# A hybrid decoder trunk on one NeuronCore: three HGRN weight blocks as three float32r products in place of one float32 product, and new rooms for the first projection weights

## The chip, the core and the metric

The kernel runs on one core of a Trainium2 chip. TensorE (PE) multiplies, VectorE (DVE) and ScalarE (ACT) do elementwise work, GpSimd (POOL) and SyncE (SP) issue most of the DMAs. The metric is the device time of one execution in microseconds (us), the median of several runs.

## The reference

Two layers of a decoder trunk for 320 tokens (256 of one prompt, 64 of eight samples), 1024 channels, float32. Each layer is a first feed-forward block, a mixer and a second feed-forward block:

```
x += 0.5 * post1(SwiGLU1(pre1(x)))
x += postm(Mix(prem(x)))
x += 0.5 * post2(SwiGLU2(pre2(x)))

Mix(u):  proj = u @ w_in                       # columns: A, B, C and three merge gates
  oa = rwkv7(A)      # 8 heads of 64, handled as 4 pairs
  ob = rglru(B)      # scan
  oc = hgrn2(C)      # 4 heads of 128, chunked, norm, gate
  merged = ga*(oa @ proj_a) + gb*(ob @ proj_b) + gc*(oc @ proj_c)
  return merged @ w_out
```

## The kernel before

All activations are kept transposed, as eight tiles of 128 channels by 320 tokens. The weights are packed in the order of use into blocks of 128 x 2048 float32 (1 MB), `wstream`; 110 blocks a layer. Blocks 0 to 33 are the first feed-forward layer, 34 to 41 the input columns of RWKV, 42 to 53 those of RG-LRU and HGRN, 54 to 57 and 58 to 65 (`B_G0`, `B_G1`) the merge gates, 66 to 71 (`B_PROJ`) the three branch projections, 72 to 75 `w_out`, 76 on the second feed-forward layer. Two SBUF buffers, `raw0` for even and `raw1` for odd blocks, take turns; SP loads a block as soon as its buffer is given back.

A block is multiplied in one of two ways. In the *float32* way (`pieces`, L607) a tile is one float32 matmul straight from `raw` and the normed input `u`; the trace records each such matmul as two. In the *float32r* way the weight and the input are each split into a high part (a copy rounded to float32r) and a low part (the difference), and a tile is three float32r matmuls: high by high, high by low, low by high. ACT makes a high part by a Copy, DVE a low part by a subtraction. The feed-forward layers, the RWKV columns, the projections and `w_out` go this way with both parts made just before use (L703, L557).

Eleven of the twelve blocks of RG-LRU and HGRN columns, the *turn* blocks (`turn_pieces`, L642), go this way with a detour. Their low parts are made during the first feed-forward layer, half a block at a time: POOL loads a half into `u` (free then), ACT makes the high part in `wha` (`presplit_hi`), DVE the low part over it (`presplit_lo`), and POOL stores that in DRAM, in `split_store`. In the mixer SP loads a raw half (512 KB) into the lower half of a `raw` buffer and the stored low half (512 KB) beside it, ACT turns the raw half into the high part in place (`turn_high`), and PE multiplies. A half's buffer is reloaded when PE has done the half, so at most two halves, one in each buffer, are there. The inputs' high parts are `nh` (it lies over `x`, which waits in DRAM meanwhile), the low parts `nl`, six tiles in `wha` and two in `ovr`.

The mixer's work on PE is interleaved by hand: `dense_part(n)` issues n tiles of weight product between the small matmuls of the recurrences. During the four HGRN heads (`hgrn_head`) these are the eight blocks 58 to 65, two a head, 16 tiles a block, all in the float32 way. In heads 0 to 2 they are issued in runs of 3, 1, 1, 1, 1, 2, 2, 2, 2, 3, 1, 2, 1, 1, 3 and 6 tiles, in head 3 in runs of 3, 1, 1, 1, 1, 2, 2, 2, 2, 3, 3 and 11. In a head's first part seven level steps alternate: DVE scales operands (`factors`), PE multiplies them (L917), DVE keeps a masked part of the result (`keep`, L1927). Then come a transposition (L922), state products (L933), the output (L947), a norm (L951), and the next head's first transposes (L906).

After head 3 PE goes on with the projections, in halves of a block (`high` on ACT, `low_half` on DVE, L557 on PE). The split parts of each half have a *room* in SBUF by a table, `half_homes`; the first four halves, 14 to 17, of blocks 66 and 67, use (`WB0`,`LO`), (`WB1`,`SS`), (`WA0`,`U0`), (`WA1`,`U1`). `WA` is in `wha`, which is also the HGRN state buffer `hs`/`hsn`; `WB` is `whb`, which is also the small weights `sw`; `U` is in `u`; `LO` is in the last tiles of `ov`; `SS` is the RWKV state buffer.

Of the kernel before, what the change touches and what calls it, by code (L numbers as in the profile page):

```python
# [70 lines left out]
NLOAD = (NBLK - (B_G0 - B_B)) // 2  # L71
# [75 lines left out]
def trunk(nc, xT, wstream, smallw, params, logits, consts, st_shift, st_rwkv, st_lru, st_conv, st_hgrn,  # L147
          yT, o_shift, o_rwkv, o_lru, o_conv, o_hgrn):
    ctx = ExitStack()
    with ctx:  # L150
# [12 lines left out]
        split_store = nc.dram_tensor("split_store", (L * NSPLIT, P, 1024), F32).ap()  # L163
# [20 lines left out]
        rt = sb("rt", T)  # L184
        rs = sb("rs", T)
# [101 lines left out]
        nl = [wha[:, T * k:T * k + T] for k in range(6)] + [ovr[:, 0, :], ovr[:, 4, :]]  # L287
# [10 lines left out]
        def split_half(h):  # L298
# [10 lines left out]
        block_done full_done half_done half_hi half_lo branch_hi branch_lo merged_hi merged_lo x_new x_first uh_first u_first sq_ready sq_added sq_last first_done hi_ready lo_ready uh_ready sum_done rt_ready u_ready u_half u_full nh_ready nl_ready x_spilled x_back turn_done turn_hi presplit silu_ready h_ready  # L309
# [14 lines left out]
        pre_loaded, pre_hi, pre_lo, pre_stored, turn_loaded, low_loaded = (  # L324
            [sem(f"{n}{h}") for h in range(2)]
            for n in ("pre_loaded", "pre_hi", "pre_lo", "pre_stored", "turn_loaded", "low_loaded"))
# [32 lines left out]
        def wait_full(eng, l, j):  # L359

            eng.wait_ge(S["full_done"], l * (B_PROJ - B_G0) + (j - B_G0 + 1))

        def wait_turn(eng, l, g):

            eng.wait_ge(S["turn_done"], l * NTURN + (g + 1))

        def landed(l, pair):

            return (l * NLOAD + pair - ((B_G0 - B_B) // 2 if 2 * pair >= B_G0 else 0)) * 16 + 16

# [10 lines left out]
        def _(sp):  # L381
# [18 lines left out]
            for l in range(L):  # L400
# [17 lines left out]
                for g in range(NSPLIT):  # L418
# [8 lines left out]
                    sp.wait_ge(S["presplit"], l * NSPLIT + g + 2)  # L427
                    sp.dma_start(parts[s][:, 1024:2048].bitcast(F32), split_store[l * NSPLIT + g, :, :])\
# [3 lines left out]
                for j in range(B_G0, B_F2 + 2):  # L432
# [5 lines left out]
                    if j == B_G0 + 1:  # L438
# [14 lines left out]
        def _(pool):  # L453
# [13 lines left out]
            for l in range(L):  # L467
# [9 lines left out]
                order = mixer_order()[B_B - B_A:][:NSPLIT // 2]  # L477
                for q in range(len(order) + 1):
                    for h in range(2):
                        g = l * NSPLIT + 2 * (q - 1) + h  # L480
                        if q:
                            pool.wait_ge(pre_lo[h], l * len(order) + q)
# [57 lines left out]
        def _(pe):  # L540
# [3 lines left out]
            def block_in(l, half, s):  # L544

                pe.wait_ge(w_loaded[s], landed(l, half))
# [67 lines left out]

            def turn_pieces(l, p):
# [3 lines left out]
                def some(n):  # L619

                    for i in range(done[0], done[0] + n):
# [4 lines left out]
                        if g >= NSPLIT:  # L626
                            if i % 16 == 0:
                                pe.wait_ge(turn_loaded[0], (l * (NTURN // 2) + g // 2) * 16 + 16)
# [6 lines left out]
                        if i % 8 == 0:  # L635
                            pe.wait_ge(S["turn_hi"], l * NSPLIT + g + 1)
                            pe.wait_ge(low_loaded[g % 2], (l * (NSPLIT // 2) + g // 2) * 16 + 16)
# [256 lines left out]
            def hgrn_head(l, p):  # L894
# [3 lines left out]
                dense_part = pieces(l, B_G1 + 2 * p, Q_G1 + 2 * p)  # L898
# [146 lines left out]
        def _(act):  # L1045
# [53 lines left out]
            def split_hi(l, i, j, s, f):  # L1099

                act.wait_ge(w_loaded[s], i * 16 + landed(l, ((B_F1, B_F2)[f] + j) // 2))
# [3 lines left out]
            def read_pair(l, j, s, dst, f, n=2):  # L1105
# [3 lines left out]
                elif j < B_G0:  # L1109
                    wait_turn(act, l, 2 * (j - B_B) + 1)  # L1110
                else:
# [3 lines left out]
            def presplit_hi(l, i):  # L1115

                for h in range(2):
                    act.wait_ge(pre_loaded[h], l * (NSPLIT * 8) + i * 16)
                    act.wait_ge(S["presplit"], l * NSPLIT + i * 2 - 1)
                    fn(pre_high[h], pre_raw[h], ACT.Copy).then_inc(pre_hi[h], 1)  # L1120
# [1075 lines left out]
```

## Time and profile before

| | us |
|---|---|
| median of 3 runs | 2081.37 |
| the runs | 2078.1, 2081.37, 2081.72 |
| the profiled execution's own time | 2080.08 |
| its span | 2078.3 |
| HGRN heads of layer 0 / layer 1, to the first projection matmul | 602.93 to 721.88 / 1631.26 to 1748.66 |

The profile is one execution. The span begins with the first instruction and ends with the last; 1.8 us lie around it. In the profile's rows a time is counted from the span's start. A matmul's recorded length reaches into the next one's, so what a matmul costs is read from start to start, not from its length. Rows of one kind in a stretch are merged by the timeline into one, with their count behind an x and the time from the first one's start to the last one's end.

### The profile page before, as it was taken

To read this page: it belongs to the slowest core of one execution; us is meant where nothing else is said; L and a number is where in the kernel's file an instruction comes from. 1 tells how busy PE (TensorE), PEld (TensorE's weight loads), DVE (VectorE), ACT (ScalarE), POOL (GpSimd) and SP (SyncE) were. 2 spreads that over 40 slices of the span, in tenths; PEclk is the share of its full clock that TensorE was granted. 3 is DMA by queue.
4 is the path that set the end of the run, shared out by engine and by line. 5 is a ranking of instruction groups with operands and counts; after the bars stand their busy time and mean duration, and the time that the engine had idled before them with its cause. 6 is when DMAs were issued, how large, how long until landed. Compare 5 with 4: busy or idle time off the path is not lost.

```text
span 2078.3 us, 31983 instructions
## 1 busy us (share of the span) xinstructions
PE 2037.3 (98%) x12928; PEld 1868.1 (90%) x12928; DVE 1379.3 (66%) x2053; ACT 797.3 (38%) x940; POOL 86.1 (4%) x164
## 2 busy tenths in 40 slices
PE   7999999999999999999999999999999999999998
PEld 6999989888877798999999998989887778989998
DVE  5776487877667676555377755877874676766544
ACT  4444463333243244233354444623323323443332
POOL 1111000000000000000011100000000000000000
PEclk9999999999999999999999999999999999999999
DMA  6887423333332342444458864323333333434442
GB/s 239 304 308 266 172 107 108 113 113 112 125 122 104 123 174 102 143 160 151 167 193 309 297 241 160 129 88 113 113 113 132 107 122 143 142 115 148 161 146 102
DMA packets 60826, 326.66 MB, mean 157 GB/s; under 512 B 7249, under 2 KB 7441, under 8 KB 34481
## 3 DMA queue, kind: packets, MB, share of 16 engines
q1 hardware_dynamic: 43200, 262.92, 35.9%
q0 software_dynamic: 17520, 62.27, 8.2%
q8 instruction: 75, 1.23, 0.2%
q14 instruction: 31, 0.25, 0.0%
HBM read 290.81 MB, written 34.36 MB: 156 GB/s over the span
## 4 chain that ended last, share of the span: by engine, by line
PE 92%; DVE 4%; DVEq 1%; ACT 1%; DMA 1%; issue 1%; SPq 0%
PE dps L703 44%; PE dps L607 11%; PE dps L557 10%; PE dps L642 6%; PE mx L803 2%; PE mx L817 2%; PE mx L813 2%; PE mx L917 2%; PE mx L659 1%; PE dps L630 1%; DMA raw<-in_wstream 1%; DVE ho L1422 1%; PE mx L933 1%; PE mx L760 1%; PE mx L970 1%; PE mx L947 1%
## 5 line engine op out<-in xcount | busy, mean ns | idle before, releaser
L1047 ACT ACTIVATE whi<-raw 128x2048 fp32r<-128x2048 f32 (+1 forms) x144 | 269.1, 1869 | 486.2 <-PE dps L703 465.0
L1419 DVE TENSOR_TENSOR wlo<-raw,whi 128x2048 fp32r<-128x2048 f32 x136 | 311.7, 2292 | 210.2 <-ACT whi L1047 205.2
L703 PE MATMUL dps<-uh,whi 128*128 128x320 f32 x1408 | 430.3, 306 | 19.6 <-DVE wlo L1419 15.0
L703 PE MATMUL dps<-uh,wlo 128*128 128x320 f32 x1408 | 434.3, 308 | 0.0
L703 PE MATMUL dps<-ul,whi 128*128 128x320 f32 x1408 | 432.9, 307 | 0.0
L703 PEld LDWEIGHTS dps<-uh,whi 128*128 128x128 f32 x1408 | 264.8, 188 | 25.1 <-issue 18.4
L703 PEld LDWEIGHTS dps<-uh,wlo 128*128 128x128 f32 x1408 | 264.8, 188 | 0.0
L703 PEld LDWEIGHTS dps<-ul,whi 128*128 128x128 f32 x1408 | 264.0, 187 | 0.6
L607 PE MATMUL dps<-u,raw 128*128 128x320 f32 x768 | 234.5, 442 | 0.0
L703 PE MATMUL dps<-hfh,whi 128*128 128x320 f32 x704 | 220.4, 313 | 0.0
L703 PE MATMUL dps<-hfh,wlo 128*128 128x320 f32 x704 | 217.6, 309 | 0.0
L703 PE MATMUL dps<-hfl,whi 128*128 128x320 f32 x704 | 216.7, 308 | 0.0
L642 PE MATMUL dps<-nh,parts 128*128 128x320 f32 x704 | 211.0, 342 | 0.0
L607 PEld LDWEIGHTS dps<-u,raw 128*128 128x128 f32 x768 | 137.9, 191 | 50.6 <-issue 5.3
L703 PEld LDWEIGHTS dps<-hfl,whi 128*128 128x128 f32 x704 | 133.2, 189 | 0.6
L703 PEld LDWEIGHTS dps<-hfh,whi 128*128 128x128 f32 x704 | 132.3, 188 | 0.6
L703 PEld LDWEIGHTS dps<-hfh,wlo 128*128 128x128 f32 x704 | 132.0, 187 | 0.0
L642 PEld LDWEIGHTS dps<-nh,parts 128*128 128x128 f32 x704 | 126.8, 189 | 4.1 <-issue 2.9
L1047 ACT ACTIVATE tmp<-mx 128x640 f32<-128x640 f32 (+2 forms) x80 | 47.4, 592 | 194.8 <-PE mx L803 127.7
L1422 DVE TENSOR_TENSOR ov<-dps,ov 128x640 f32<-128x640 f32 x52 | 42.8, 823 | 71.9 <-PE dps L703 65.9
L1047 ACT ACT_TABLE_LOAD x64 | 82.1, 1283 | 2.1 <-PEq L2177 0.7
L1422 DVE TENSOR_TENSOR ov<-dps,rs 128x640 f32<-128x640 f32 x56 | 46.2, 824 | 54.3 <-PE dps L703 45.3
(321 smaller groups left out, 3493.3 us busy)
## 6 DMA issues: line engine op xcount, KB each, us to landing
raw<-in_wstream SPq DMA_DIRECT2D x198, 1024.0 KB, 4.8
u<-in_wstream POOLq DMA_DIRECT2D x44, 512.0 KB, 7.1
split_store<-wha POOLq DMA_DIRECT2D x44, 512.0 KB, 7.6
raw<-in_wstream SPq DMA_DIRECT2D x44, 512.0 KB, 4.1
parts<-split_store SPq DMA_DIRECT2D x44, 512.0 KB, 5.0
hs<-in_st_hgrn POOLq DMA_DIRECT2D x8, 512.0 KB, 5.6
out_o_hgrn<-hs POOLq DMA_DIRECT2D x8, 512.0 KB, 2.9
out_yT<-x SPq DMA_DIRECT2D x2, 1280.0 KB, 4.5
```

The source lines that it names most:

```text
L557: m = pe.matmul(out, w[:, k, n0:n0 + P], v[:, k, :], start=first and i == 0, stop=last and i == 2, skip_group_check=True)
L607: m = pe.matmul(dps[:, 2 * s + c, 0:T], w[:, k, c * P:(c + 1) * P], u[:, k, :], start=k == 0, stop=k == KD - 1, skip_group_check=True)
L630: m = pe.matmul(dps[:, 2 * (b % 2) + c, 0:T], w[:, k, c * P:(c + 1) * P], u[:, k, :], start=k == 0, stop=k == KD - 1, skip_group_check=True)
L642: m = pe.matmul(dps[:, 2 * (b % 2) + c, 0:T], w[:, k % 4, c * P:(c + 1) * P], v, start=k == 0 and t == 0, stop=k == KD - 1 and t == 2, ski ...
L703: m = pe.matmul(dps[:, 2 * half + c, 0:T], w[:, k, c * P:(c + 1) * P], v[:, k0 + k, :], start=first and k == 0 and i == 0, stop=last and k ...
L803: m = pe.matmul(mx01[:, c * P:(c + 1) * P], ao[li % 2][:, c, :], tinv[:, c, :], start=True, stop=True)
L813: m = pe.matmul(mx23[:, c * P:(c + 1) * P], tinvt[:, c, :], zs[:, c, :], start=True, stop=True)
L817: m = pe.matmul(product_at(li, c), zs[:, c, :], tinvt[:, c, :], start=True, stop=True)
L917: m = pe.matmul(mx[0:b - a, (li + 1) % 2, a:b], kss[li % 2][:, a:b], qps[li % 2][:, a:b], start=True, stop=True)
L1047: return nc.scalar.activation(out, in_, f, **kw)
L1419: return nc.vector.tensor_tensor(out, a, b, op)
L1422: return nc.vector.tensor_tensor(out, a, b, ALU.mult)
```

## The change

- `B_LATE` = 63: the last three gate blocks, 63, 64 and 65, become six *late halves* e = 0 to 5. Their low parts are made in the first feed-forward layer behind those of the turn blocks, in its down projection (ACT after steps 3, 5 and 7, DVE after steps 5, 7 and 9), and stored by POOL. `split_store` grows from 22 to 28 halves a layer.
- PE takes them in `late_pieces`: a tile of these blocks is three float32r matmuls. Before each half PE waits for the high part, the low part's landing and `nl_moved`.
- SP loads a raw half and a low half for each e. Halves 0, 2 and 4 go to `raw1`, 1 and 3 to `raw0`, half 5 to `LO` and `SS`. Half 0 waits for block 61, half 1 for block 62, half e from 2 on for half e - 2. The reload of `x` moves from before block 56 to behind block 67's load and waits for half 5.
- ACT makes the high parts in `late_high`: 0 before and 1 behind the copy of the second transposition in head 2, 2 between head 2's two gate reads; 3 and 4 before and 5 behind that copy in head 3.
- HGRN needs `wha`, so after the third gate read ACT copies the six tiles of `nl` from `wha` to `whb` (128 x 1920); the other two now lie over the norms' scratch rows `rt` and `rs`. POOL's state load waits for the copy. With it a wait of DVE for the shift output goes (`low_normed(6, 8)`).
- The projections' first halves get the rooms (`U0`,`U1`), (`LO`,`SS`), (`WA0`,`WB0`), (`WA1`,`WB1`). In head 3 ACT makes half 14's high part as before, but half 15's only after the two gate reads; DVE makes half 14's low part before the norm's reciprocal instead of behind all heads.

```diff
+B_LATE = B_PROJ - 3
+NLATE = 2 * (B_PROJ - B_LATE)
+NALL = NSPLIT + NLATE
-    last = [("WB0", "LO"), ("WB1", "SS"), ("WA0", "U0"), ("WA1", "U1")]
+    last = [("U0", "U1"), ("LO", "SS"), ("WA0", "WB0"), ("WA1", "WB1")]
...
+        nl, nl_late = ([v[:, T * k:T * k + T] for k in range(6)] + [rt_low[:, :], rs_low[:, :]] for v in (wha, whb))
+        late_raw = ov[:, 60:64, :].rearrange("p a t -> p (a t)")[:, 0:1024]
...
+        def late_rooms(e):
+            if e == NLATE - 1:
+                return late_raw, rooms["LO"], rooms["SS"]
+            s = 1 - e % 2
+            return raw[s][:, 0:1024], parts[s][:, 0:1024], parts[s][:, 1024:2048]
...
                     pool.wait_ge(S["oc_ready"], n + 1)
+                    pool.wait_ge(S["nl_moved"], l + 1)
                     pool.dma_start(hs[:, :, :], st_hgrn[bass.ds(n, 1)].rearrange("a p b v -> (a p) b v"))\
...
+                        if i % 8 == 0:
+                            pe.wait_ge(S["nl_moved"], l + 1)
+                            pe.wait_ge(S["turn_hi"], l * NALL + NSPLIT + e + 1)
+                            pe.wait_ge(low_loaded[e % 2], (l * (NALL // 2) + (NSPLIT + e) // 2) * 16 + 16)
+                        hi, low = (v.rearrange("p (k n) -> p k n", k=4) for v in late_rooms(e)[1:])
+                        for t, (w, v) in enumerate(((hi, nh[:, k, :]), (hi, nl_late[k]), (low, nh[:, k, :]))):
+                            m = pe.matmul(dps[:, 2 * (b % 2) + c, 0:T], w[:, k % 4, c * P:(c + 1) * P], v,
...
-                    if f == 0 and j == 1:
-                        presplit_hi(l, KF // 2)
+                    if f == 0 and j in (1, 3, 5, 7):
+                        presplit_hi(l, KF // 2 + j // 2)
...
-                    if f == 0 and j == 3:
-                        presplit_lo(l, KF // 2)
+                    if f == 0 and j in (3, 5, 7, 9):
+                        presplit_lo(l, KF // 2 + j // 2 - 1)
...
+                act.wait_ge(S["lg_done"], l * 2 + 2)
+                wait_turn(act, l, NSPLIT - 1)
+                fn(whb[:, 0:6 * T], wha[:, 0:6 * T].bitcast(F32), ACT.Copy).then_inc(S["nl_moved"], 1)
                 act.wait_ge(S["ob_ready"], l + 1)
...
-                dve.wait_ge(S["shift_out_ready"], l + 1)
                 low_normed(6, 8)
```

SP's queue from the load of block 62 to that of block 68. Before (block 62 is the first row; L388 is a block's load):

```order
L388 DMA raw0<-in_wstream 128x2048 [waits full_done]
L388 DMA raw1<-in_wstream 128x2048 [waits full_done]
L388 DMA raw0<-in_wstream 128x2048 [waits full_done]
L388 DMA raw1<-in_wstream 128x2048 [waits full_done]
L388 DMA raw0<-in_wstream 128x2048 [waits full_done]
L388 DMA raw1<-in_wstream 128x2048 [waits full_done]
L388 DMA raw0<-in_wstream 128x2048 [waits half_lo]
```

After, from half 2 on (L458 loads a raw half, L461 a low half, L472 `x`):

```order
L458 DMA raw1<-in_wstream 128x1024 [waits turn_done]
L461 DMA parts1<-split_store 128x1024 [waits presplit]
L458 DMA raw0<-in_wstream 128x1024 [waits turn_done]
L461 DMA parts0<-split_store 128x1024 [waits presplit]
L458 DMA raw1<-in_wstream 128x1024 [waits turn_done]
L461 DMA parts1<-split_store 128x1024 [waits presplit]
L458 DMA ov<-in_wstream 128x1024 [waits ss_free,turn_done]
L461 DMA wss<-split_store 128x1024 [waits presplit]
L400 DMA raw0<-in_wstream 128x2048 [waits turn_done]
L400 DMA raw1<-in_wstream 128x2048 [waits turn_done]
L472 DMA x<-out_yT 128x2560 [waits x_spilled,turn_done]
L400 DMA raw0<-in_wstream 128x2048 [waits half_lo]
```

Loads of whole blocks have become pairs of half loads, each of which waits for PE's matmuls on the half before the last (`turn_done`), and the load of `x` now stands in this queue.

ACT's queue at head 2's end and in head 3, from the norm's root of head 2 (`tmp<-mx,epst`). Before:

```order
L1047 ACTIVATE tmp<-mx,epst 128x320 [waits om_done]
L1047 ACT_TABLE_LOAD
L1047 ACTIVATE ov<-dps 128x640 [waits full_done] x2
L1047 ACTIVATE sq<-mx 128x256 [waits ht_done]
L1047 ACTIVATE sq<-mx 64x128
L1047 ACTIVATE sq<-mx 128x256 [waits ht_done]
L1047 ACTIVATE sq<-mx 64x128
L1047 ACTIVATE ho<-mx 128x320 [waits o_done]
```

After:

```order
L1108 ACTIVATE tmp<-mx,epst 128x320 [waits om_done]
L1108 ACT_TABLE_LOAD
L1108 ACTIVATE ov<-dps 128x640 [waits full_done]
L1108 ACTIVATE parts1<-raw1 128x1024 [waits turn_loaded0]
L1108 ACTIVATE ov<-dps 128x640 [waits turn_done]
L1108 ACTIVATE sq<-mx 128x256 [waits ht_done]
L1108 ACTIVATE sq<-mx 64x128
L1108 ACTIVATE parts0<-raw0 128x1024 [waits turn_loaded1]
L1108 ACTIVATE parts1<-raw1 128x1024 [waits turn_loaded0]
L1108 ACTIVATE sq<-mx 128x256 [waits ht_done]
L1108 ACTIVATE sq<-mx 64x128
L1108 ACTIVATE ovr<-ov 128x1024 [waits turn_loaded1]
```

Four copies that wait for DMAs (halves 2, 3, 4 and 5) now stand between the copies that PE's small matmuls wait for.

PE at the start of head 3, from its first transpose. Before:

```order
L906 MATMUL mx<-cst,tmp 128x128 [waits hsig_ready,osd_ready]
L906 MATMUL mx<-cst,tmp 128x128
L906 MATMUL mx<-cst,tmp 64x128
L607 MATMUL dps<-u,raw0 128x320 [waits pair_free0,w_loaded0]
L607 MATMUL dps<-u,raw0 128x320 x2
L911 MATMUL mx<-tmp 128x128 [waits hq_ready]
L911 MATMUL mx<-tmp 128x128
L911 MATMUL mx<-tmp 64x64
```

After:

```order
L967 MATMUL mx<-cst,tmp 128x128 [waits hsig_ready,osd_ready]
L967 MATMUL mx<-cst,tmp 128x128
L967 MATMUL mx<-cst,tmp 64x128
L668 MATMUL dps<-nh,parts1 128x320 [waits turn_hi,low_loaded0,nl_moved,pair_free0]
L668 MATMUL dps<-whb,parts1 128x320
L668 MATMUL dps<-nh,parts1 128x320 x2
L668 MATMUL dps<-whb,parts1 128x320
L668 MATMUL dps<-nh,parts1 128x320 x2
L668 MATMUL dps<-whb,parts1 128x320
L668 MATMUL dps<-nh,parts1 128x320
L972 MATMUL mx<-tmp 128x128 [waits hq_ready]
```

The three tiles between the transposes and the first level product, one matmul each, are nine matmuls, and the first of them waits for half 2's two parts.

## Rows read from the trace of the kernel before

**Rows 1.** The page: PE's busy share, and the chain that ended last, by engine

```profile
PE 2037.3 (98%) x12928; PEld 1868.1 (90%) x12928; DVE 1379.3 (66%) x2053; ACT 797.3 (38%) x940; POOL 86.1 (4%) x164
PE 92%; DVE 4%; DVEq 1%; ACT 1%; DMA 1%; issue 1%; SPq 0%
```

**Rows 2.** Timeline (start, length, engine, line, out<-in, count), head 2, layer 0

```profile
682.72 0.81 PE L607 MATMUL dps<-u,raw 128*128 128x320 f32 x2
683.36 0.95 PE L947 MATMUL mx<-tmp,hs 128*128 128x8 f32 x8
...
687.84 3.39 PE L607 MATMUL dps<-u,raw 128*128 128x320 f32 x12
...
691.07 0.49 PE L906 MATMUL mx<-cst,tmp 128*128 128x128 f32 x3
```

**Rows 3.** Timeline, PE, float32r matmuls: the feed-forward layer, then one turn tile

```profile
19.90 0.31 PE L703 MATMUL dps<-ul,whi 128*128 128x320 f32 x1
...
21.35 0.31 PE L703 MATMUL dps<-uh,wlo 128*128 128x320 f32 x1
...
419.01 0.39 PE L642 MATMUL dps<-nh,parts 128*128 128x320 f32 x1
...
419.54 0.33 PE L844 MATMUL mx<-uu,tmp 128*128 128x64 f32 x2
```

**Rows 4.** Timeline, where half 2 will be loaded, and an ACT copy of a turn half

```profile
317.00 1.08 ACT L1047 ACTIVATE parts<-raw 128x1024 fp32r<-128x1024 f32 x1
...
685.60 1.86 PE L607 MATMUL dps<-u,raw 128*128 128x320 f32 x6
...
691.26 0.33 SPq L388 DMA_DIRECT2D raw<-in_wstream  x1
```

**Rows 5.** The lines L424 (raw halves) and L428 (low halves): issue to landing

```profile
L424 SPq DMA_DIRECT2D raw<-in_wstream x44: 327/328/430, 312.4 to 1558.7; - x44
DMA to landing us min/median/max: 3.8/4.1/7.0
L428 SPq DMA_DIRECT2D parts<-split_store x44: 427/432/663, 312.7 to 1559.1; - x44
DMA to landing us min/median/max: 4.8/5.0/7.8
```

**Rows 6.** Timeline, head 3 of layer 0: the level steps on PE and DVE

```profile
693.91 0.44 DVE L1927 COPY_PREDICATED ho<-cst,mx 128x256 f32<-128x256 uint32 x1 [1.04 <-PE mx L911]
...
695.65 0.43 DVE L1927 COPY_PREDICATED ho<-cst,mx 128x256 f32<-128x256 uint32 x1
...
704.08 0.90 DVE L1422 TENSOR_TENSOR tmp<-tmp 128x320 f32<-128x320 f32 x2
...
704.86 0.49 PE L922 MATMUL mx<-cst,tmp 128*128 128x128 f32 x3
```

**Rows 7.** Timeline, head 3's end and the projections' start; last row: layer 1

```profile
712.60 3.22 PE L607 MATMUL dps<-u,raw 128*128 128x320 f32 x6
...
716.20 6.09 PE L607 MATMUL dps<-u,raw 128*128 128x320 f32 x22
721.88 0.70 PE L557 MATMUL dps<-ovr,whb 128*128 128x320 f32 x2
...
729.36 0.30 PEld L557 LDWEIGHTS dps<-ovr,wha 128*128 128x128 f32 x2 [0.35 <-DVE ulo L1419]
...
1740.74 1.86 PE L607 MATMUL dps<-u,raw 128*128 128x320 f32 x6
```

**Rows 8.** Stretches: PE, PEld, DVE, ACT, POOL busy (instructions), granted clock, DMA share, GB/s

```profile
712.50:714.00 1.50, 1.50 (x5) 1.11 (x5) 0.00 (x0) 1.20 (x3) 0.00 (x0) 0.50 0.87 350
```

**Rows 9.** Timeline: cover in the first feed-forward layer, and in head 0

```profile
192.32 2.35 DVE L1419 TENSOR_TENSOR wha<-u,wha 128x1024 fp32r<-128x1024 f32 x2
...
209.47 2.29 DVE L1419 TENSOR_TENSOR wlo<-raw,whi 128x2048 fp32r<-128x2048 f32 x1 [4.75 <-ACT whi L1047]
...
605.77 0.44 DVE L1927 COPY_PREDICATED ho<-cst,mx 128x256 f32<-128x256 uint32 x1 [5.24 <-PE mx L911]
```

More of the change, by code:

```diff
@@ L431, in _ @@
                 sp.dma_start(raw[1][:, :], wstream[l * NBLK + order[B_G0 - 1 - B_A], :, :]).then_inc(turn_loaded[0], 16)
-                for j in range(B_G0, B_F2 + 2):
+                for j in range(B_G0, B_LATE):
                     if j < B_G0 + 2:
@@ L437, in _ @@
                     load(l, 0, j - j % 2, j % 2)
-                    if j == B_G0 + 1:
+                for e in range(NLATE):
+                    if e < 2:
+                        wait_full(sp, l, B_LATE - 2 + e)
+                    else:
+                        wait_turn(sp, l, NTURN + e - 2)
+                    if e == NLATE - 1:
+                        sp.wait_ge(S["ss_free"], (l + 1) * HP + 1)
+                    whole, _, low = late_rooms(e)
+                    sp.dma_start(whole, wstream[l * NBLK + B_LATE + e // 2, :, 1024 * (e % 2):1024 * (e % 2) + 1024])\
+                        .then_inc(turn_loaded[e % 2], 16)
+                    sp.wait_ge(S["presplit"], l * NALL + NSPLIT + e + 2)
+                    sp.dma_start(low.bitcast(F32), split_store[l * NALL + NSPLIT + e, :, :])\
+                        .then_inc(low_loaded[e % 2], 16)
+                for j in range(B_PROJ, B_F2 + 2):
+                    if j < B_PROJ + 2:
+                        wait_turn(sp, l, NTURN + NLATE - 3 + j - B_PROJ)
+                    else:
+                        raw_free(l, j)
+                    load(l, 0, j - j % 2, j % 2)
+                    if j == B_PROJ + 1:
+                        wait_turn(sp, l, NTURN + NLATE - 1)
                         sp.wait_ge(S["x_spilled"], l * 16 + 16)
@@ L544, in block_in @@
             def block_in(l, half, s):
-                pe.wait_ge(w_loaded[s], landed(l, half))
+                pe.wait_ge(w_loaded[s], landed(l, half, s))
             def pair_wait(l, qhalf, s):
@@ L613, in pieces, with late_pieces, some @@
                 return some
+            def late_pieces(l, p):
+                done, whole = [0], pieces(l, B_G1 + 2 * p, Q_G1 + 2 * p)
+                def some(n):
+                    for i in range(done[0], done[0] + n):
+                        b, part, c, k = B_G1 + 2 * p + i // 16, i // 8 % 2, i // 4 % 2, i // 8 % 2 * 4 + i % 4
+                        if b < B_LATE:
+                            whole(1)
+                            continue
+                        e = 2 * (b - B_LATE) + part
+                        if i % 16 == 0:
+                            pair_wait(l, (Q_G1 + b - B_G1) // 2, b % 2)
+                        if i % 8 == 0:
[5 more added lines that the diff above has]
+                            m = pe.matmul(dps[:, 2 * (b % 2) + c, 0:T], w[:, k % 4, c * P:(c + 1) * P], v,
+                                          start=k == 0 and t == 0, stop=k == KD - 1 and t == 2, skip_group_check=True)
+                        if i % 8 == 7:
+                            m.then_inc(S["turn_done"], 1)
+                    done[0] += n
+                return some
             def turn_pieces(l, p):
@@ L1287, in hgrn_head @@
                         .then_inc(pair_free[s], 1)
+                    if p == 2 and s == 0:
+                        late_high(l, 2)
+                if p == 3:
+                    high(l, H_PROJ + 1)
             sqrt_table()
```

85 lines of the change are left out of this document (49 added, 36 removed).

## The prediction, made before the run

> **What bounds the kernel now.** I read the page first: PE is busy 98% of the span and makes 92% of the chain that ended last [rows 1]. So a gain must come from PE's own time, and it counts only where no other engine is the next to finish. The timeline of PE therefore decides, read from start to start. In heads 2 and 3 of HGRN the float32 tiles fill the gaps between small matmuls. A single one moves PE from 682.72 to 683.36, 0.64 us; six of them (12 records) from 687.84 to 691.07, 3.23, or 0.54 a tile [rows 2]. The float32r way: ten matmuls of the feed-forward layer take 1.45 (19.90 to 21.35), 0.145 each, so a further tile of three costs 0.435, and a single tile between small matmuls takes PE from 419.01 to 419.54, 0.53 [rows 3]. I price a run of n tiles at 0.53 + 0.435 (n - 1): 0.97, 1.40, 2.71 and 4.88 us for 2, 3, 6 and 11 tiles. Only 48 tiles a layer change, so the bare gain is 48 x 0.105 = 5.0 us a layer.
>
> The second thing to see is where DVE is the bound. In head 3's level steps DVE keeps a result at 693.91 after a last wait of 1.04; the next keep comes at 695.65, and it goes on with no idle time shown until it scales the last operand at 704.08, whose first half is there at 704.53. PE's transposition follows at 704.86 [rows 6]. In this loop a faster tile saves nothing but its last run.
>
> **Head 2, part by part** (times of layer 0). Block 62 stays float32; the 16 tiles of block 63 lie behind the loop. In the run of 3 that covers the transposition two change: 1.62 to 0.54 + 0.97, 0.11 saved. The three single tiles save 0.11 each, the pair 1.08 - 0.97 = 0.11. The run of 3 saves 1.62 - 1.40 = 0.22, the run of 6 saves 3.23 - 2.71 = 0.52. Sum 1.29. The other engines' waits in this part are for ACT copies and DVE products that start from PE's own results, so they move along.
>
> **Head 3's start: a new wait.** Half 2 goes to `raw1`, which half 0 holds. Half 0 ends with the first tile of the run at 685.60 [rows 4], 0.55 earlier by the savings so far: 685.60 + 0.53 - 0.55 = 685.6. SP issues 0.19 after PE's last matmul (691.07 to 691.26 at a block's end) [rows 2, 4]: 685.8. The raw half lands 4.1 later; the low half, issued 0.33 later, takes 5.0 [rows 5]: 689.9 and 691.1. ACT's copy takes 1.08 [rows 4] and is ready at 691.0. PE would arrive at 691.39 (the transposes start at 691.07 and take 0.32) less 1.29, at 690.1. So PE stands for 1.0 us, and of head 2's 1.29 only 0.3 is left. The wait's bounds: none, if PE is held up elsewhere by as much; 3.8, if the landings take the longest times in the rows, 7.0 and 7.8 [rows 5]. I take the medians, since no other DMA is in flight then in the profile. In front of that queue nothing else waits: SP's next command, half 3, has until PE's ninth tile.
>
> **Head 3.** The three tiles before the level steps save 0.22. The loop is DVE's and gives nothing for its seven runs; its last run of two saves 0.11. Then the run of 3 (the transposition's cover) 0.22, the run of 3 behind the output 0.22, and the run of 11: 716.20 to 721.88 is 5.68 [rows 7], against 4.88, 0.80. Sum 1.57. Are the halves in time? Half 4 waits for the eighth tile, the first of the fifth step's two. Seven steps take 10.6 us (693.91 to 704.53), so that tile ends some 5.9 us before PE wants half 4, at the second tile of the transposition's cover; the pair takes 0.19 + 0.33 + 5.0 = 5.5 [rows 5, 6]. The slack is about 0.3 us, and ACT's copies for the transposition stand in its queue behind half 4's copy. Half 5 is loaded when half 3 is done, near the transposition at 704.86, is whole some 6 us later and is wanted 3 tiles into the last run, after 716.20 [rows 7]. Half 3 has the whole of the loop before it.
>
> **The projections.** Half 16's wait of 0.35 in layer 0 [rows 7] goes, since block 67 now loads when half 4 is done, eight tiles earlier. For layer 1 I take half of it, between none and all. Half 15 is new on the edge: ACT reads the last gates only when half 5 is done (shorter than its 1.08 copy), then copies (1.08 [rows 4]), then DVE subtracts (half of 2.35 [rows 9]), 3.3 us; PE's 24 matmuls of half 14 take 24 x 0.145 = 3.5. I cost it at nothing. `x` and block 68 now load later, one behind the other; block 68 is needed only after halves 14 to 17, 4 x 3.5 = 14 us.
>
> **What is added elsewhere.** In the first feed-forward layer DVE subtracts two more halves, 2.35 us, after three steps, ACT copies as much; a step there shows DVE idle 4.75 before its 2.29 product [rows 9]. Cost nothing; uncovered it would be at most 3 x 2.35 a layer. POOL's three more rounds of loads and stores end within the down projection, and its next command waits for the mixer. With it SP's block loads share the DMA engines in the down projection as they do now in the loop before it. The copy of `nl` (128 x 1920, 1.9 by two copies of 1024 at 1.08 each) delays head 0's first functions; DVE idles 5.24 before the first keep of head 0 [rows 9], so it is hidden. The dropped shift wait was long met.
>
> **The sum.** Per layer 0.3 + 1.57 + 0.35 (0.17 in layer 1): 2.2 and 2.1, 4.3 us in all, of 10 us bare: 2080.08 - 4.3 = 2075.8 against the profiled execution. The median of the runs is 1.3 above that execution and one run is 2.0 below it; I put the reference halfway, at 2080.7, and predict **2076.4**.
>
> The Trainium skill, "TensorE: Matmul & The Clock Gate", section "Wait — 56ns, not 53.3ns?", gives a matmul's start to start as its columns over 2.4 GHz plus about 2.5 ns: 136 ns for 320 columns, so that a float32r tile would be 0.41. Rows 3 have 0.145 for it, 9 ns more, so here the measured row decides. By the page a tile would save 0.13 instead of 0.105, and the sum would come to about 5.5 us.
>
> **The rivals.**
> *Nearly the whole gain.* No wait at head 3's start, because PE loses time elsewhere in head 2 or the half lands as fast as 3.8 and 4.8 [rows 5] and the reload starts earlier. Then 1.29 + 1.57 + 0.3 a layer: 6.3 us, 2074.4. For it: 44 such pairs in the turn stage never show PE waiting. Against: there the same two-half scheme has longer recurrences between halves.
>
> *The clock takes it back.* In head 3 of layer 0 the granted clock is 0.50, the 1.2 GHz level, from 712.5, after a stretch of PE's narrow state and output products without tiles [rows 8]. Six records take 3.22 there and 1.86 in layer 1 at 2.4 GHz [rows 7], a loss of 1.4 us. If a stop of 1.0 at head 3's start and shorter fillers bring such a fall in both heads 3 and at both starts, three falls more, 4.2 us, the gain is gone: 2080.6. For it: it has happened once in two such heads. Against: at the start of head 3 wide products stand on both sides. The Trainium skill says, in "TensorE: Matmul & The Clock Gate", section "Part 1: The HAM clock gate", that the low clock is the default and activity lifts it; by that rule less filler is a risk here, and the trace's fall behind narrow work agrees.
>
> *Slower: late halves.* Every half has its buffer only when the half before the last is done. If landings behave as the longest rows (7.0 and 7.8 for a pair, 2.8 more), half 2 costs PE 2.8 more, half 4 misses by 2.5 and holds ACT's transposition copy too: 5.3 a layer, 10.6 in all, against a gain of 4.3: 2087.0. It decides at about 1.2 us more per landing. For it: half 4's slack is 0.3 us. Against: the long rows are those where four half loads were issued within 1.4 us.
>
> *The change does nothing for PE,* because the filler only covers DVE's and ACT's chains everywhere: 2080.7. Against it speak the runs of 6 and 11, which have no such chain.
>
> **How the numbers follow.** Forecast (2074.9 to 2077.9, by waits 0.7 longer or shorter a layer): 0.5. Nearly the whole gain: 0.13. Clock or nothing: 0.25. Late halves, whole or in part: 0.12. The run of this kernel can be told from no change at about 0.2%, 4.2 us, which is just inside the forecast's own 4.3; I split it evenly. Faster: 0.25 + 0.13, rounded to 0.4. Slower: 0.1. The same: 0.5. The range takes in the whole gain and the lost one and a part of the late halves: 2073.3 to 2082.5.
>
> **What would show it.** In the changed profile PE should stand about 1 us before head 3's first tile (released by ACT or the low half's DMA), and nowhere else in heads 2 and 3 for more than 0.3; the run of 11 should take 4.9; DVE's level steps should keep their lengths; the first projection matmul should come 1.9 us earlier after block 62's end; PE should have no new wait in the feed-forward layers. Wrong would be: a wait at half 4 or half 15, DVE waiting in the loop, or more low-clock stretches than one.

## The result: slower by 0.2%, and the profile after

| | before | changed |
|---|---|---|
| median, us | 2081.55 (22 runs) | 2086.19 (22 runs, 2083.31 to 2094.05) |
| ratio to before, 95% interval | | 1.002 (1.0014 to 1.0027) |
| profiled execution / its span, us | 2080.08 / 2078.3 | 2087.11 / 2085.3 |

The prediction was 2076.4, faster, with a range of 2073.3 to 2082.5; the median lies above the range. The kernel became slower by 4 to 5 us in the median, and by 7.0 us from trace to trace. The page of the changed kernel, PE's and the chain's lines, and one group of the feed-forward layer (idle time before it behind the last bar), against [rows 1]:

```profile
PE 2035.4 (98%) x13024; PEld 1878.2 (90%) x13024; DVE 1393.8 (67%) x2065; ACT 824.1 (40%) x966; POOL 98.9 (5%) x188
PE 87%; DVE 5%; DMA 4%; ACT 2%; DVEq 1%; issue 1%; POOL 0%; SPq 0%; ACTq 0%; POOLq 0%
L764 PE MATMUL dps<-hfh,whi 128*128 128x320 f32 x704 | 222.3, 316 | 7.3 <-DVE wlo L1503 7.3
```

PE is down from 92% to 87% of the chain, DMA is up from 1% to 4%. The last row is new in kind: PE stands 7.3 us in front of the down projection's matmuls.

To find the place I read off PE's timeline where each stage starts and took the differences (L0 and L1 are the two layers; the L0 value of the first stage also holds the program's start, which varies by about 1 us):

| stage on PE, us | before L0 / L1 | changed L0 / L1 | difference |
|---|---|---|---|
| first feed-forward layer, to its last sum | 253.02 / 243.82 | 259.16 / 248.94 | +6.14 / +5.12 |
| from there to the mixer's last sum | 541.40 / 539.19 | 538.04 / 538.30 | -3.36 / -0.89 |
| of it head 2 | 29.38 / 29.38 | 28.13 / 27.80 | -1.25 / -1.58 |
| of it head 3 | 30.81 / 29.14 | 30.07 / 30.40 | -0.75 / +1.26 |
| second feed-forward layer | 243.86 / 243.86 | 243.87 / 243.86 | 0.01 / 0.01 |

The differences add up to the 7.0 us of the spans. The mixer gained 4.25 us in this execution, close to the sum that was forecast. Some of that closeness is luck: in nine traces of kernels with the same mixer code (the changed kernel's, and those of the experiments up to "How much each round costs") the two mixers gain between 2.3 and 7.4 us against the one trace of before, 4.3 on average. The first feed-forward layer, where the low parts are made, lost 11.3.

**What happened there.** The timeline of ACT in layer 0's down projection of the changed kernel (start, length, instruction, idle time before it and what ended it). `wha<-u` is a round's high part, `whi<-raw` the high part of the feed-forward layer's own next block:

```profile
199.95 1.92 ACT L1108 ACTIVATE whi<-raw 128x2048 fp32r<-128x2048 f32 x1 [3.76 <-PE dps L764]
207.01 2.01 ACT L1108 ACTIVATE wha<-u 128x1024 fp32r<-128x1024 f32 x2 [5.14 <-POOLq L523]
208.92 1.90 ACT L1108 ACTIVATE whi<-raw 128x2048 fp32r<-128x2048 f32 x1
...
221.70 2.01 ACT L1108 ACTIVATE wha<-u 128x1024 fp32r<-128x1024 f32 x2 [6.15 <-POOLq L523]
223.61 1.90 ACT L1108 ACTIVATE whi<-raw 128x2048 fp32r<-128x2048 f32 x1
...
235.91 2.01 ACT L1108 ACTIVATE wha<-u 128x1024 fp32r<-128x1024 f32 x2 [6.36 <-POOLq L523]
239.23 3.73 ACT L1108 ACTIVATE whi<-raw 128x2048 fp32r<-128x2048 f32 x2
```

Line 523 is POOL's count that the previous round's two stores have landed; only then may ACT write `wha` again. Three times ACT stands 5 to 6 us for it, and its queue is in order, so the own block's high part stands behind the round. The Trainium skill, "Perfetto Trace Analysis", section "Tensor Engine Instruction (MATMUL, LD_WEIGHTS)", says as much: ACT's, DVE's and GpSimd's queues are strictly in order; these rows agree. The same high parts in the kernel before:

```profile
207.52 1.92 ACT L1047 ACTIVATE whi<-raw 128x2048 fp32r<-128x2048 f32 x1 [5.12 <-PE dps L703]
...
219.84 1.92 ACT L1047 ACTIVATE whi<-raw 128x2048 fp32r<-128x2048 f32 x1 [3.76 <-PE dps L703]
...
233.52 1.92 ACT L1047 ACTIVATE whi<-raw 128x2048 fp32r<-128x2048 f32 x1
239.20 1.92 ACT L1047 ACTIVATE whi<-raw 128x2048 fp32r<-128x2048 f32 x1 [3.75 <-PE dps L703]
```

The changed program was 0.53 us earlier at that point. With this taken off, the high parts behind the three rounds come 1.9, 4.3 and 6.2 us late: 208.92, 223.61 and 239.23 against 206.99, 219.31 and 232.99. The lateness grows by some 2 us a round mainly because rounds follow each other in 14.7 and 14.2 us (207.01, 221.70, 235.91), while two steps of PE take 12.9 on average (three steps from 219.84 to 239.20 are 19.4). Behind the third round two short pieces of ACT's own work come first, so its high part starts at 239.23 and not at 237.8. DVE's low part for the last of these blocks starts at 241.18, and PE's timeline shows the end of it:

```profile
240.65 0.31 PE L764 MATMUL dps<-hfh,wlo 128*128 128x320 f32 x1
243.53 0.63 PE L764 MATMUL dps<-hfh,whi 128*128 128x320 f32 x1 [2.57 <-DVE wlo L1503]
243.96 0.47 PE L764 MATMUL dps<-hfl,whi 128*128 128x320 f32 x1
244.23 0.47 PE L764 MATMUL dps<-hfh,wlo 128*128 128x320 f32 x1
```

After the wait the matmuls follow each other in 0.27 us instead of 0.145: PE runs at the lower of its two clocks (1.2 GHz, a granted clock of 0.5). PE in stretches of the changed kernel (length, busy, instructions, granted clock, DMA share, GB/s), layer 0 and then layer 1:

```profile
235.00:240.00 5.00, 5.00 (x36) 1.00 0.66 275
240.00:245.00 5.00, 2.43 (x12) 0.84 0.55 195
245.00:250.00 5.00, 5.00 (x30) 0.82 0.93 354
250.00:255.00 5.00, 5.00 (x35) 1.00 0.73 262
...
1270.00:1275.00 5.00, 2.86 (x18) 0.92 0.55 216
1275.00:1280.00 5.00, 5.00 (x27) 0.74 0.82 287
```

In the kernel before these stretches have a granted clock of 1.00. In layer 0 the waits are 4.4 us (three: 1.03, 0.83 and 2.57), in layer 1 2.9 (0.47, 0.26 and 2.14). Only the longest of each layer is followed by a slow stretch, which costs about 1.6 us; that is most of the 1.7 and 2.2 us that each layer loses beyond its waits.

### The profile page after: what moved, and what is told of

Its sections match the earlier page's. It is cut to its first block, busy times and chain, and to the rows that moved or that the text cites. A ratio compares the mean times of both kernels' runs of the same rounds, so it can differ in the third digit from the quotient of the medians.

```text
span 2085.3 us, 32351 instructions
## 1 busy us (share of the span) xinstructions
PE 2035.4 (98%) x13024; PEld 1878.2 (90%) x13024; DVE 1393.8 (67%) x2065; ACT 824.1 (40%) x966; POOL 98.9 (5%) x188
## 3 DMA queue, kind: packets, MB, share of 16 engines
q8 instruction: 76, 1.25, 0.2%
## 4 chain that ended last, share of the span: by engine, by line
PE 87%; DVE 5%; DMA 4%; ACT 2%; DVEq 1%; issue 1%; POOL 0%; SPq 0%; ACTq 0%; POOLq 0%
PE dps L764 39%; PE dps L590 11%; PE dps L640 8%; PE dps L703 6%; DMA split_store<-wha 3%; PE mx L864 2%; PE dps L668 2%; PE mx L878 2%; PE mx L874 2%; PE mx L978 1%; PE mx L720 1%; PE dps L691 1%; DVE ho L1506 1%; PE mx L994 1%; PE mx L821 1%
## 5 line engine op out<-in xcount | busy, mean ns | idle before, releaser
L640 PE MATMUL dps<-u,raw 128*128 128x320 f32 x576 | 173.8, 439 | 0.0
L640 PEld LDWEIGHTS dps<-u,raw 128*128 128x128 f32 x576 | 103.1, 190 | 37.8 <-issue 3.0
L1108 ACT ACTIVATE parts<-raw 128x1024 fp32r<-128x1024 f32 x54 | 56.9, 1054 | 74.7 <-DMA raw<-in_wstream 74.6
```

The lines of the kernel that those rows point to most:

```text
L640: m = pe.matmul(dps[:, 2 * s + c, 0:T], w[:, k, c * P:(c + 1) * P], u[:, k, :], start=k == 0, stop=k == KD - 1, skip_group_check=True)
L1108: return nc.scalar.activation(out, in_, f, **kw)
```

## Experiments

My theory (A): ACT's in-order wait for the round trip of the previous round's store is the loss. The rivals: (B) the added transfers take bandwidth from the block loads; (C) the added work of ACT and DVE is itself too much for the down projection.

### No rounds

The rounds of the late blocks go, the mixer stays.

```diff
-order = mixer_order()[B_B - B_A:][:NSPLIT // 2] + list(range(B_LATE, B_PROJ))
+order = mixer_order()[B_B - B_A:][:NSPLIT // 2]
...
-if f == 0 and j in (1, 3, 5, 7):
-    presplit_hi(l, KF // 2 + j // 2)
+if f == 0 and j == 1:
+    presplit_hi(l, KF // 2)
```

> Left out: the three rounds for the late blocks in the first feed-forward layer (their loads, ACT's and DVE's work, their stores); the late blocks' low halves are read from the first six stored halves, so the late blocks' output is not the reference's, and every mixer instruction stays. All theories of where the loss sits agree here, so this run only tests the place: the profile of the changed kernel has the first feed-forward layer 6.2 and 5.1 us later in the two layers, and about 4.3 us won in the mixer. If the rounds are the whole loss: about 2077 us (2076 to 2078), faster than before, and the span from the start to the first layer's last sum at 253.0 us again. If the mixer itself loses time at full speed: 2080 or more.

Measured: 2075.36 us, ratio 0.9967 (0.9956 to 0.9978), the first stage 253.24 / 243.80. That is a little below the 2076 to 2078 expected. The place is right. The mixer's change alone brings about 6.9 us by the ratio (4.6 to 9.2 by its interval), and 4.6 from trace to trace: 5.1 won in the two mixers, 0.6 lost in the program's start and the last feed-forward layer. Forecast were 4.3 for the whole change.

### Work without transfers, transfers without work

In the first, POOL's loads and stores of the late rounds are cut to 8 columns. In the second they are whole, one round after the other, but ACT and DVE do nothing for them.

```diff
+                        elif q < len(order):
+                            pool.dma_start(pre_raw[h][:, 0:8], wstream[l * NBLK + order[q], :, 0:8]).then_inc(pre_loaded[h], 16)
...
+                        elif q:
+                            pool.dma_start(split_store[g, :, 0:8], pre_high[h].bitcast(F32)[:, 0:8]).then_inc(pre_stored[h], 16)
```

> The three late rounds keep ACT's copies, DVE's subtractions and all their waits, but POOL's loads and stores for them move 8 columns instead of 1024, so their round trip is short; the late low halves are read from the first six stored halves, so the late blocks' output is not the reference's. Theory A (ACT waits in order for the previous round's store, 5.1 to 6.4 us of idle three times a layer, and the next high parts come late): about 2077 us. Theory B (the added transfers take share from the block loads): about 2077 us too. Theory C (ACT's 2 us and DVE's 2.4 us per round are themselves too much for the down projection): 2085 us or more, PE's waits for DVE's low parts at line 764 still near 7 us in six.

Measured: 2075.73 us, 0.9967 (0.9955 to 0.9979); first stage 253.07 / 243.80. All of ACT's and DVE's extra work is there and costs nothing: C falls, and that part of the prediction (DVE and ACT have room) was right.

> The three late rounds keep POOL's loads and stores at full size, one after the other, but ACT and DVE do nothing for them and wait for nothing of them; the stored halves hold other data, so the late blocks' output is not the reference's. Theory A (ACT's in-order wait): about 2077 us, since the wait is gone. Theory B (transfers take share from the block loads): 2083 us or more, with longer landings of the block loads and ACT waiting for blocks. Theory C (the work itself): about 2077 us.

Measured: 2075.6 us, 0.9967 (0.9955 to 0.9979); first stage 253.16 / 243.79. All bytes are moved and cost nothing: B falls. Work and transfers are each free; only their coupling costs.

### Two rooms

Everything is computed. The late rounds take turns between `wha` and `whb` for the high part; the small weights, which want `whb`, are loaded after the last round.

```diff
+pre_late = [whb[:, 1024 * h:1024 * h + 1024] for h in range(2)]
...
-act.wait_ge(S["presplit"], l * NALL + i * 2 - 1)
-fn(pre_high[h], pre_raw[h], ACT.Copy)
+back = 0 if not isinstance(i, int) or i <= NSPLIT // 2 else 2
+act.wait_ge(S["presplit"], l * NALL + i * 2 - 1 - back)
+fn(pre_room(i, h), pre_raw[h], ACT.Copy)
```

> Everything is computed. The late rounds take turns between two rooms for their high parts, so ACT may start a round when the store of the round before the last has landed, not the last one. The load of a round still follows DVE's subtraction of the one before. Theory A (the store's round trip in front of ACT): 2077 to 2078 us, ACT's waits ahead of the late rounds under 1 us each, line 764 without waits of over 0.5 us. Theory B and theory C: no change against the changed kernel, 2085 to 2087 us. If the load's landing is as late as the store's, the waits move from the store to the load and 2082 to 2086 us follow.

Measured: 2077.22 us, 0.9977 (0.9967 to 0.9986); first stage 254.06 / 244.93. The rounds' copies on ACT's timeline of this kernel:

```profile
202.14 2.08 ACT L1123 ACTIVATE whb<-u 128x1024 fp32r<-128x1024 f32 x2
215.81 2.01 ACT L1123 ACTIVATE wha<-u 128x1024 fp32r<-128x1024 f32 x2
228.54 1.99 ACT L1123 ACTIVATE whb<-u 128x1024 fp32r<-128x1024 f32 x2
```

None waits for POOL any more. The same work and the same bytes, with the dependence on the last store gone (and the small weights loaded later), give the gain back: A holds. Of the 1.1 us left in layer 1, 0.9 are a new wait of PE for ACT's squares.

### Which leg of the round trip

Of the diff with 8 columns above, the first kernel has only the cut of the stores, the second only that of the loads.

> The late rounds keep ACT's and DVE's work, all waits and POOL's full loads (1024 columns), but their stores move 8 columns; the late low halves are read from the first six stored halves, so the late blocks' output is not the reference's. If the store is the leg of the round trip that ACT waits behind: 2076 us, no PE wait at line 764's matmuls for DVE. If the load is the long leg (it is issued ahead of the store on the same queue, so it lands with or before it): 2081 to 2086 us, and ACT's idle ahead of the late copies ends at the load of u.

Measured: 2077.07 us, 0.9971 (0.9959 to 0.9983); first stage 254.13 / 244.51. That is near the first branch, with one wait of PE for DVE's low parts left in each layer, 0.5 us.

> The mirror of the run above: the late rounds' loads move 8 columns, their stores stay full. The late low halves are read from the first six stored halves, so the late blocks' output is not the reference's. If the store's own landing is the long leg: ACT still waits behind POOL's count, but the store no longer shares the queue with a load of its size, so a part of the loss stays: 2078 to 2084 us. If only load and store together are too long for two steps of the down projection: 2076 us, ACT's waits ahead of the late copies under 2 us each.

Measured: 2074.83 us, 0.9966 (0.9954 to 0.9978); first stage 253.85 / 243.79. This is the last branch: neither leg alone is the long one. Issue to landing of the late rounds' full stores, in layer 0 of the changed kernel (L519) and of the kernel with short loads (L524), then two of ACT's rounds of the latter:

```profile
L519 POOL DMA_DIRECT2D split_store<-wha x6: 532/537/539, 210.1 to 239.7; - x6
DMA to landing us min/median/max: 3.1/5.5/10.3
```

```profile
L524 POOL DMA_DIRECT2D split_store<-wha x6: 534/539/539, 207.5 to 234.5; - x6
DMA to landing us min/median/max: 4.6/5.0/6.0
```

```profile
203.13 1.99 ACT L1113 ACTIVATE wha<-u 128x1024 fp32r<-128x1024 f32 x2
...
229.53 1.99 ACT L1113 ACTIVATE wha<-u 128x1024 fp32r<-128x1024 f32 x2
```

With small loads beside them the stores land within 5.1 us, and in up to 10.3 when two loads of 512 KB, issued in turn with the stores, share the queue. The last round's stores have no load of POOL beside them in either kernel; they take 5.9 and 6.0 us in the kernel with short loads and 3.1 and 3.2 in the changed one, so the queue's own loads are not all that counts.

In the kernel with short stores ACT waits 4.58 us before the first late round and 0.38 before the second. The 4.58 don't belong to a short store: that round waits for the stores of the last turn round, which are whole in this kernel (11.4 us for the later one). In the kernel with short loads these same stores land within 4.5 us, and ACT does not wait for them. The short stores, behind full loads, are the second of these lines, the loads in front of them the first (window 205 to 225):

```profile
DMA to landing us min/median/max: 4.8/6.2/7.1
DMA to landing us min/median/max: 4.4/5.8/6.7
```

Each store of 8 columns is issued 0.5 us behind a load and lands 0.1 to 0.2 us after it. The Trainium skill, "DMA: Bandwidth & Descriptors", section "Queues, rings and completion order", says that a transfer's semaphore update lands only after every earlier write of the same DMA engine; these rows fit that, though they don't prove the mechanism, and the page says it in its part on SP's and ACT's queues, while these are POOL's.

### How much each round costs

Two, and then one, of the three late rounds are kept; for two:

```diff
-order = mixer_order()[B_B - B_A:][:NSPLIT // 2] + list(range(B_LATE, B_PROJ))
+order = mixer_order()[B_B - B_A:][:NSPLIT // 2] + list(range(B_LATE, B_LATE + 2))
...
-if f == 0 and j in (1, 3, 5, 7):
+if f == 0 and j in (1, 3, 5):
```

> The changed kernel with the third late round left out, two of three kept whole, one room for the high parts; late low halves are read from the first six stored halves, so the late blocks' output is not the reference's. No late round: 2075.4 us; three: 2086.2. If each round loses the same (3.6 us of the 10.8): 2082.6 us. If the down projection has a reserve that the first rounds use up and only the last late high parts reach TensorE (in the changed kernel the longest wait, 2.57 us, is the last one, at 243.5): under half of the loss, 2077 to 2080 us.

> As the run before, with only the first late round kept. If each round loses the same: 2079.0 us. If there is a reserve: 2075.4 to 2076 us, no wait of TensorE at the down projection's matmuls for DVE's low parts.

| late rounds | 0 | 1 | 2 | 3 |
|---|---|---|---|---|
| ratio to before | 0.9967 | 0.9981 | 0.9995 | 1.002 |
| 95% interval | 0.9956 to 0.9978 | 0.9972 to 0.9990 | 0.9986 to 1.0005 | 1.0014 to 1.0027 |
| median, us | 2075.36 | 2078.23 | 2082.05 | 2086.19 |
| first stage L0 / L1, us | 253.24 / 243.80 | 253.44 / 244.87 | 255.79 / 245.09 | 259.16 / 248.94 |

Waits of the kernel with one round (first two rows, layer 1) and with two rounds (last two, layer 0): engine, line and releaser, us, times, longest.

```profile
ACT wha L1110 <- POOLq L523: 4.9, 1, 4.9
PE dps L766 <- DVE wlo L1505: 0.8, 1, 0.8
```

```profile
ACT wha L1110 <- POOLq L523: 10.8, 2, 5.9
PE dps L766 <- DVE wlo L1505: 1.6, 2, 0.9
```

Neither expectation was met cleanly. By the stage, the first round costs 1.3 us over both layers, the second 2.6, the third 7.2: a reserve is used up (in the rows of before ACT waits 4 to 5 us for PE ahead of most blocks), and then the loss grows. By the ratios the steps are 2.9, 2.9 and 5.2 us, nearly even at first, but the intervals reach about 2 us to either side and don't tell 1.3 from 2.9. The traces with one and two rounds also lost in the heads: with one round a head 1 took 31.07 instead of 29.38, with two head 3 took 31.63 and 30.48 against 30.10 and 29.40 with none. All three ran in part at a granted clock of 0.5, and so did the 30.10. These are stages whose code is the same; whether such stretches come by chance or follow from the shift in time I could not settle.

### Two late blocks, rounds three steps apart

```diff
-B_LATE = B_PROJ - 3
+B_LATE = B_PROJ - 2
...
-if f == 0 and j in (1, 3, 5, 7):
-    presplit_hi(l, KF // 2 + j // 2)
+if f == 0 and j in (1, 4, 7):
+    presplit_hi(l, KF // 2 + j // 3)
```

> Everything is computed. Only the last two HGRN weight blocks are done as three float32r products, so two late rounds a layer, and they stand three steps apart in the down projection (18 us) instead of two (12 us); head 2 is as before and nothing is waited for at head 3's start. If a round (about 14.5 us with its landings) only has to fit between two calls: ACT's waits go, and of the mixer's 4.3 to 5.5 us the part of block 63 (1.3 us less 1.0 for its wait, a layer) is missing while its wait is too: 2077 to 2078 us. If any third-step round still delays the high parts: 2080 us or more.

Measured: 2090.62 us, 1.0041 (1.0028 to 1.0055). The expectation failed, but not in the feed-forward layer: its first stage is 253.62 / 243.79, ACT waits for no store, so two full rounds with one room fit when they are three steps apart. The loss is at the projections' start, from my own regrouping of the halves (first row PE's wait in layer 0, 4.9 in layer 1; then the chain):

```profile
PE dps L590 <- ACT ov L1108: 4.5, 1, 4.5
```

```profile
713.71 1.34 PE dps L668 x9
715.05 0.02 issue
715.07 4.76 DMA raw<-in_wstream
```

With four late halves the load of block 66 waits for the third of them, and behind it PE has only eight tiles (3.5 us) left, less than the load's 4.76 and ACT's work behind it: PE waits for ACT's reading of the gates, which stands in ACT's queue behind the copy of half 14, and that waits for block 66. In the changed kernel with six halves that load waits for the fourth, sixteen tiles before the end. It resembles the "late halves" rival of the prediction, but what comes late is the first projection block, by the choice of its buffer, and no late half.

### Half 2 of the late blocks in the room of `u`

Two rooms as above, and the third late half is loaded into `u` once block 62 is done.

```diff
+            if e == 2:
+                return uflat[:, 0:1024], rooms["U0"], rooms["U1"]
```

> Everything is computed. Two rooms for the late high parts in the feed-forward layer as in the run with two rooms (2077.2 us), and in the mixer the third late half is loaded into u's room as soon as block 62 is done, instead of waiting for the turn rooms. If the 1.0 us that TensorE waits at head 3's start (longest single wait for the stored low parts) is paid in full by the run: 2 us less than the run with two rooms, 2075 us. If DVE's run of 11 blocks behind it sets head 3's end anyway: under 0.5 us less, 2077 us.

Measured: 2076.28 us, 0.9966 (0.9952 to 0.9979). Against two rooms alone 0.9 less in the median, which the intervals don't tell apart. PE's waits at head 3's start, layer 0:

```profile
PE dps L692 <- ACT ulo L1132: 1.0, 1, 1.0
```

The wait is as long as it was and has another releaser. So this edit did not take the wait away, and its price remains untested. The kernel computes everything and beats both the kernel before and the changed one, whose interval begins at 1.0014.

### Two rooms, rounds three steps apart

The late rounds stand behind ACT's steps 4, 7 and 10 of the down projection instead of 3, 5 and 7, and DVE's behind 6, 9 and 11.

> Everything is computed. Two rooms for the late high parts, and the rounds three steps of the down projection apart instead of two, so the last one stands behind the last feed-forward block's high part. With two rooms already enough, spacing brings nothing in the down projection: 2077 us if the last store lands before ACT wants the room for the first weights of the recurrent layer, as it does in the two-rooms run. If that store (about 10 us after DVE's last low parts) now holds up those weights: the loss goes from the down projection to the start of the recurrent layer, 2080 to 2088 us.

Measured: 2087.25 us, 1.0023 (1.0014 to 1.0032): the second branch. ACT's timeline at the end of layer 0's first stage:

```profile
240.30 1.99 ACT L1123 ACTIVATE whb<-u 128x1024 fp32r<-128x1024 f32 x2
252.61 1.06 ACT L1123 ACTIVATE wha<-raw 128x1024 fp32r<-128x1024 f32 x1 [10.31 <-POOLq L536]
```

The last round now ends so late that ACT stands 10.3 us before the first weights of the next stage, and the squares behind them hold PE for 4.2. What it waits for is POOL's count of all stores (line 1253 of this kernel), and the last to be counted is not a store of `wha`:

```profile
233.49 0.54 POOL L530 DMA_DIRECT2D split_store<-wha  x1
...
245.28 0.53 POOL L530 DMA_DIRECT2D split_store<-whb  x1 [0.60 <-DVE whb L1519]
```

The last store from `wha`, the room that the weights want, lands 11.4 us after its issue, at 244.9; ACT writes at 252.61, when the store from `whb` has landed (7.2 us). So this run shows that the last store's count must not come late. Whether spaced rounds would fit with a count of their own for `wha` is untested.

## Why the prediction was wrong, point by point

- **"What is added elsewhere. Cost nothing"** is the step that failed, by 11.3 us. I costed ACT's and DVE's work, which is free (work without transfers), and the transfers' bandwidth, which is free too (transfers without work). I left out ACT's wait for the stores of the round before, and what is queued behind it. The prediction's own sign for this, "PE should have no new wait in the feed-forward layers", failed. So did the one on low-clock stretches: beside the program's end the trace has four, two in the heads 3 and two behind the stops. "SP's block loads share the DMA engines as they do now in the loop before it" looked at the share of the engines and not at the pace: in that loop a round fits only just. The rows of before, ACT's rounds in the loop, and then the landing of POOL's stores there (L487, window 30 to 180):

```profile
141.81 2.00 ACT L1047 ACTIVATE wha<-u 128x1024 fp32r<-128x1024 f32 x2
155.99 2.01 ACT L1047 ACTIVATE wha<-u 128x1024 fp32r<-128x1024 f32 x2 [0.23 <-POOLq L491]
169.54 2.00 ACT L1047 ACTIVATE wha<-u 128x1024 fp32r<-128x1024 f32 x2
...
DMA to landing us min/median/max: 7.3/8.3/9.3
```

  and of the changed kernel, the last store of a late round, and the landings of the stores issued from 193.8 to 226.0:

```profile
211.28 0.54 POOL L519 DMA_DIRECT2D split_store<-wha  x1
...
DMA to landing us min/median/max: 5.4/9.0/11.9
```

  In the loop rounds follow each other in 13.9 us on average, and ACT already waits for the count there, 0.23 us once in layer 0 and 1.4 once in layer 1. In the down projection a round gets 12.9 and needs 14.7: ACT's two copies and DVE's, shifted by one copy (from 207.01 to the last store's issue at 211.28, 4.3), and 10.4 to its landing. So the pace is 1 us shorter, and the last store of a round takes 9.8 to 11.9 us where it took at most 9.3 in the loop; why it lands later there is not shown.
- **"Uncovered it would be at most 3 x 2.35 a layer"** was meant as the bound. The loss of 6.1 and 5.1 us stayed under its 7.05, but only by luck, since it comes from waits that have nothing to do with DVE's 2.35. The lateness that adds up from round to round (1.9, 4.3, 6.2 us) is what a bound had to follow.
- **Head 2, -1.29:** right. It gained 1.25 in layer 0 and 1.58 in layer 1, where head 1 just before took 0.26 longer.
- **The wait at head 3's start, 1.0:** right in size and releaser. PE and DVE in head 3 of the changed kernel, layer 0:

```profile
696.68 0.38 PE L668 MATMUL dps<-nh,parts 128*128 128x320 f32 x1 [1.01 <-DMA parts<-split_store]
```

```profile
698.98 0.45 DVE L2009 COPY_PREDICATED ho<-cst,mx 128x256 f32<-128x256 uint32 x1 [1.29 <-PE mx L972]
...
709.17 0.89 DVE L1506 TENSOR_TENSOR tmp<-tmp 128x320 f32<-128x320 f32 x2
```

- **Head 3, DVE's loop gives nothing:** right. From the first keep to the last scaling it took 10.17 us in [rows 6] and takes 10.19 here. Halves 4 and 5 and half 15 are in time; PE waits for no other half.
- **Head 3 as a whole:** before, layer 1 took 29.14 at the full clock; less 1.57 and plus 1.0 that is 28.57. The kernel with short loads, whose mixer is the changed kernel's, took 28.53 and 28.96. In the changed kernel itself both heads 3 have a slow stretch (PE, PEld, DVE, ACT and POOL busy, granted clock):

```profile
718.00:721.40 3.40, 3.40 (x13) 3.00 (x12) 0.00 (x0) 2.56 (x3) 0.00 (x0) 0.52 0.40 158
...
1748.00:1752.00 4.00, 4.00 (x17) 3.61 (x17) 0.00 (x0) 2.76 (x5) 0.00 (x0) 0.58 0.63 256
```

  Before it was one of two [rows 8]. The clock rival therefore came true in part, in this execution with about 1.5 us in layer 1, and I had given it only as one of the cases for no gain. Of the 20 heads 3 of the changed kernel and of the nine kernels with the same late halves and rooms in the mixer, fifteen took 29.4 or more (up to 31.63), five under 29.1; before, 30.81 and 29.14.
- **The projections' start:** half 16's wait is gone, as forecast. From the first projection matmul to the mixer's last sum it is 71.95 in both layers instead of 72.54 and 72.62, a gain of 0.6 a layer where I had 0.35 and 0.17.
- **The rivals:** "late halves" had the right sign (2087.0) at the wrong place, so that its time is near the measured one is luck. None of the four looked at the stage where the low parts are made.

## What to carry to other kernels

When work is hung into the gaps of a loop, compare its period, not only its busy time: the time from one use of its buffer to the next, with the landing of the store that frees it, against the pace of the loop that carries it. A wait on an in-order queue costs nothing while the wait it replaces is longer; behind that, every work item that is queued after it is late, and the lateness adds up from round to round. Here a second buffer for the high part took the store out of the period and brought the gain back, with the same work and the same bytes.

## What the runs showed of the hardware that I had not expected

- A landing depends on what is in flight beside it: the stores of 512 KB land in 4.6 to 5.1 us beside small loads and in up to 10.3 beside loads of their own size, and a store of 8 columns issued 0.5 us behind a full load lands 0.1 to 0.2 us after that load.
- A stop of 2.57 us was followed by some 3 us of TensorE at the lower clock: matmuls 0.27 us apart from 243.96 to 246.63, and then 0.145 again. That made it cost about 1.6 us more than its own length; the stops of 1.03 and 0.83 us before it had no such stretch.
